# Moving one small sum later in a matmul queue, and taking another from split parts

## The chip, the cores and the metric

The kernel runs on one core of a Trainium2 chip. The metric is device microseconds (us) of one execution. The core's engines work from queues of their own and meet at semaphores: TensorE (PE for the matmuls, PEld for loading their stationary operand), VectorE (DVE), ScalarE (ACT), GpSimd (POOL) and SyncE (SP, which issues the transfers here). "PE waits for a semaphore" means that everything behind that wait in PE's queue stands still too.

## What is computed

Two layers of a decoder trunk over 256 tokens of width 1024, in float32:

```python
for i in range(2):
    x = x + 0.5 * swiglu(rms_norm(x, ffn1_norm[i]), ffn1_w_in[i], ffn1_w_out[i])
    hm = rms_norm(x, mix_norm[i])
    if i == 0: x = x + retention(hm, ret_w_in[0], ret_w_out[0])       # 4 heads, keys 256 wide, values 512
    else:      x = x + window_attention(hm, k_sh, v_sh, ...)          # 16 query heads of 64, window 128
    x = x + 0.5 * swiglu(rms_norm(x, ffn2_norm[i]), ffn2_w_in[i], ffn2_w_out[i])
    if i == 0: k_sh, v_sh = shared_kv(x, kv_norm, kv_w, k_norm)
```

`rms_norm` needs the sum of squares of each token. Inside retention each head's output is normed again by its own sum of squares (over 512 values) and gated before the output projection, which has 16 row blocks of 128: four blocks for each head.

## The kernel before

**Split operands.** Every large product is done as float32r matmuls on two parts. An operand v becomes `hi = v` rounded to float32r and `lo = v - hi`; a product is hi*hi + hi*lo + lo*hi. The activations lie as `[hi | lo]`, 512 columns, so one block of weights costs two matmuls: `w_hi` against 512 columns and `w_lo` against the first 256. The document calls these two a *pair* (`weight_block`, L1213). In *passes* means all the `w_hi` matmuls of a run first and then all of its `w_lo` ones.

**Weights.** They come in units through four slots. SP loads unit u into `stage`, ACT writes `w_hi` (`split`, L337), DVE writes `w_lo` (`split`, L652, 128x2048, one unit). ACT may write a slot only after PE has used the unit four before it (`used`).

**Norm sums.** POOL squares the tiles of x and adds them up (`square_sum`). For the norms in `PARTS` it then writes the sum as `sq_parts = [hi | lo]` (`sum_parts`: a cast, L1179, and a subtraction, L1181), and PE sums over partitions with one float32r matmul against ones. The attention's norm (ATT) isn't in `PARTS`: there PE needs the sum by token as a column, and takes it from the float32 `sq_sum` with two float32 matmuls of two columns each (four records in the trace, because a float32 matmul is two).

**The end of retention.** DVE adds up the last head's squares and writes `sq_parts` (`last_head_sum`, L969 to L974). PE sums them over partitions (`head_sum(4)`), DVE reads that (`norm_y`, L982 on), norms and gates the head, ACT writes the hi part of `y_t`, DVE the lo part (`store_y`, L998, which sets `y_lo`). Meanwhile PE does what doesn't need this head: the first 12 blocks of output tiles 0, 1 and 2 and the first 7 of tile 3 (`early`), with `head_sum(4)` behind the first tile's 12. Then it waits for `y_lo` and finishes tiles 0 to 7 in order. Tiles 0 to 3 use weight units 0 to 3 of this phase; units 4 to 7 follow in the same slots.

**The start of attention.** PE does the keys' transposes, query products, masks, the norm's column sums (`norm_sum(ATT)`) and then transposes, scores and further query products, in an order that is written out by hand in `attention` (PE). DVE, in its own written order, adds the residual tiles, splits a unit (L652), rotates the first half's queries (`q_rope(0, 1)`, L841 to L847), reads the column sums (`token_columns`, L890), computes the head scales and the softmax front (L901 to L1032, twice), splits a unit, rotates the next quarter (`q_rope(0, 0)`) and so on. PE's `q_transposes(c, t)` wait for `roped`, which `q_rope` sets.

Instructions on a matmul helper all have its line, L1211.

Of the kernel before, what the change touches and what calls it, by code (L numbers as in the profile page):

```python
# [21 lines left out]
F32R = mybir.dt.float32r  # L22
# [6 lines left out]
P = 128  # L29
T = 256  # L30
D = 1024
# [9 lines left out]
HEADS_R, DK, DV = 4, 256, 512  # L41
# [45 lines left out]
RET, ATT = 1, 4  # L87
LATE_NORMS = (0, 5)
HEAD_SUMS = HEADS_R
PARTS = {RET: 0, 2: HEADS_R + 1, 3: HEADS_R + 2, 5: HEADS_R + 3}  # L90
CREDIT = 2


def sums_before(m):

    return m + (HEAD_SUMS if m > RET else 0)


def added_for(m):

    return DT * (m + 1) + (HEAD_SUMS if m > RET else 0)
# [22 lines left out]
def trunk(nc, x_t, gains, w_in, w_out, w_ret, w_ret_out, w_kv, w_q, w_o, rot, decay, rope, head_gains,  # L124
          mask_c, sinks_c, ident_c, out):
    def at(name, shape, dtype, offset):
        return nc.alloc_sbuf_tensor_at(name, shape, dtype, offset=offset)
# [54 lines left out]
    ones = at("ones", [P, P], F32, misc + 19968)  # L182
# [3 lines left out]
    sq_sum = at("sq_sum", [P, T], F32, misc + 23552)  # L186
    sq = at("sq", [P, T], F32, misc + 24576)
    sq_parts = at("sq_parts", [P, 2 * T], F32R, misc + 23552)
    sq_all = at("sq_all", [P, T], F32, misc + 27200)
# [8 lines left out]
    ps = nc.alloc_psum_tensor("ps", [P, 8, 512], F32)  # L198
    SUM, FIRST_SUM, COLUMNS = 7, 3, 6
# [45 lines left out]
    def quarter(d):  # L245

        return d // 4, slice(d % 4 * UNIT // 4, (d % 4 + 1) * UNIT // 4)
# [22 lines left out]
    with nc.Block() as block:  # L270
# [371 lines left out]
        def _(dve):  # L642
# [25 lines left out]
            def token_sums(m):  # L668


                dve.wait_ge(sum_done, sums_before(m) + 1)
                bank = FIRST_SUM if m in LATE_NORMS else SUM
                if m == 3:
                    nc.vector.tensor_scalar(col_v[:], ps[:, COLUMNS, 0:4], V_SCALE / D, V_SCALE * EPS, ALU.mult, ALU.add)
                ins = nc.vector.tensor_scalar(n_v[:], ps[:, bank, 0:T], V_SCALE / D, V_SCALE * EPS, ALU.mult, ALU.add)
                if m in PARTS:
                    ins = add_half(ins, PARTS[m], D, bank)
                ins.then_inc(sum_read, 1)

            def token_scale(m):  # L680
# [8 lines left out]
            def add_half(ins, n, width, bank=SUM):  # L689

                ins.then_inc(half_added, 1)
                dve.wait_ge(half_added, n + 1)
                return nc.vector.scalar_tensor_tensor(n_v[:], ps[:, bank, T:2 * T], V_SCALE / width, n_v[:], ALU.mult,
                                                      ALU.add)
# [428 lines left out]
            for d in range(DT):  # L1123
                s, cols = quarter(d)
# [7 lines left out]
            for q in range(2):  # L1132
# [5 lines left out]
                cols = slice(q * UNIT // 2, (q + 1) * UNIT // 2)  # L1138
# [13 lines left out]
        def _(pool):  # L1152
            def square_sum(m):
# [4 lines left out]
                nc.gpsimd.tensor_tensor(sq_sum[:], x[:, 0, :], x[:, 0, :], ALU.mult).then_inc(sum_added, 1)  # L1158
                with pool.Fori(0, DT - 2 if m in PARTS else DT - 1) as i:

# [6 lines left out]
                    nc.gpsimd.tensor_tensor(sq_sum[:], sq_sum[:], sq[:], ALU.add).then_inc(sum_added, 1)  # L1167
                if m in PARTS:
                    pool.wait_ge(sum_added, added_for(m) - 1)
# [3 lines left out]
                    nc.gpsimd.tensor_tensor(sq_all[:], sq_sum[:], sq[:], ALU.add).then_inc(sq_added, 1)  # L1173
                    sum_parts(PARTS[m])

            def sum_parts(n):

                pool.wait_ge(sq_added, n + 1)
                nc.gpsimd.tensor_copy(sq_parts[:, 0:T], sq_all[:]).then_inc(sq_hi, 1)  # L1179
                pool.wait_ge(sq_hi, n + 1)  # L1180
                nc.gpsimd.tensor_tensor(sq_parts[:, T:2 * T], sq_all[:], sq_parts[:, 0:T].bitcast(F32),  # L1181
                                        ALU.subtract).then_inc(sum_added, 1)
# [26 lines left out]
        def _(pe):  # L1209
            def matmul(out_, w, x_, start, stop):  # L1210
                return nc.tensor.matmul(out_, w, x_, start=start, stop=stop)  # L1211
# [7 lines left out]
            def high_product(bank, slot, b, moving, first):  # L1219

                return matmul(ps[:, bank, :], w_hi[:, slot, b * P:(b + 1) * P], moving, first, False)

            def low_product(bank, slot, b, moving, last):

                return matmul(ps[:, bank, 0:T], w_lo[:, slot, b * P:(b + 1) * P], moving[:, 0:T], False, last)
# [15 lines left out]
            def norm_sum(m):  # L1241


                pe.wait_ge(sum_added, added_for(m))
                bank = FIRST_SUM if m in LATE_NORMS else SUM
                if m in PARTS:
                    last = matmul(ps[:, bank, :], ones[:].bitcast(F32R), sq_parts[:], True, True)
                elif m != ATT:
                    last = matmul(ps[:, bank, 0:T], ones[:], sq_sum[:], True, True)
                if m == 3:  # L1250
                    last = column_sums(ps[:, COLUMNS, 0:4], sq_all)
                if m == ATT:
                    last = column_sums(ps[:, SUM, T:T + 4], sq_sum)
                last.then_inc(sum_done, 1)

            def column_sums(out_, sums):

                for t in range(2):
                    last = matmul(out_[:, 2 * t:2 * t + 2], sums[:, t * P:(t + 1) * P], ones[:, 0:2], True, True)
                return last  # L1260

            def first_blocks(kt):

# [208 lines left out]
            def ret_out_in_passes(d, ks):  # L1472

                u = FIRST["ret_out", 0] + d
                pe.wait_ge(hi_ready, u + 1)
                for k in ks:
                    high_product(d, u % SLOTS, k, y_t[:, k, :], k == 0)
                pe.wait_ge(lo_ready, u + 1)
                for k in ks:
                    low_product(d, u % SLOTS, k, y_t[:, k, :], k == YT - 1)  # L1480

            def ret_out(d, ks):

                u = FIRST["ret_out", 0] + d
                pe.wait_ge(lo_ready, u + 1)
                for k in ks:
                    last = weight_block(d, u % SLOTS, k, y_t[:, k, :], k == 0, k == YT - 1)
                return last

            def retention():  # L1490
                with pe.Fori(0, 2) as i:
                    ret_head(0, i)
                    ret_head(1, i)
                three = YT - YT // HEADS_R
                early = (three, three, three, 7, 0, 0, 0, 0)

                pe.wait_ge(pair_free, 4 + 4 * HEADS_R)
                pe.wait_ge(y_lo, HEADS_R - 1)
                ret_out_in_passes(0, range(0, three - 4))
                ret_out(0, range(three - 4, three))  # L1500
                head_sum(HEADS_R)
                for d in range(1, 4):
                    ret_out(d, range(early[d]))

                pe.wait_ge(y_lo, HEADS_R)
                for d in range(DT):
                    ret_out(d, range(early[d], YT)).then_inc(used, 1)
# [272 lines left out]
```

## Time and profile before

| | |
|---|---|
| median of 3 runs | 1016.08 us (1015.81 to 1016.28) |
| the profiled execution | 1016.55 us, of which 1014.8 us from its first to its last instruction |
| PE busy | 1010.3 us |
| PEld busy | 886.1 us |
| DVE busy | 786.3 us |
| ACT busy | 496.7 us |
| POOL busy | 101.1 us |

The page gives each engine's busy time; the chain of work that ended last names, step by step, what the end waited for. A timeline lists instructions by start; neighbours of the same line and operands are merged, with their count as x2, x8. The interval from one matmul's start to the next one's is what a matmul costs PE; the recorded duration is longer, since matmuls are pipelined.

### The profile page before, as it was taken

The numbers are of one execution on the slowest core, as the hardware profiler recorded it, in microseconds if no ns is written. First come the engines' busy times: TensorE is split into PE (matmuls) and PEld (weight loads), VectorE is DVE, ScalarE is ACT, GpSimd is POOL, SyncE is SP. The second block draws the span as 40 slices with busy tenths as digits, with TensorE's granted clock in tenths as the row PEclk, the third lists the DMA queues.
The fourth block names the chain that finished last, engine by engine and source line by source line (L and its number), as shares of the span: only waits on it lengthen the run. The fifth ranks groups of instructions, "written<-read, shape, count | busy, mean of one in ns | idle before, by whom it ended". The sixth has DMA issues, their size and how long they took to land.

```text
span 1014.8 us, 15813 instructions
## 1 busy us (share of the span) xinstructions
PE 1010.3 (100%) x5914; PEld 886.1 (87%) x5914; DVE 786.3 (77%) x886; ACT 496.7 (49%) x536; POOL 101.1 (10%) x103
## 2 busy tenths in 40 slices
PE   9999999999999999999999999999999999999998
PEld 8888888888888888888888888888897898888888
DVE  7988866797797878777767797787778977977743
ACT  7455435544443364454444454465447944554432
POOL 0000013201101052000013100000220041000000
PEclk9999999999999999999999999999999999999999
DMA  9664456652552544554455645535563345544461
GB/s 350 239 233 180 142 174 216 243 202 104 218 193 98 192 175 163 208 200 170 148 189 197 249 165 195 192 140 171 185 239 120 107 160 192 207 170 163 156 191 65
DMA packets 32295, 185.31 MB, mean 183 GB/s; under 512 B 3840, under 2 KB 6400, under 8 KB 16128
## 3 DMA queue, kind: packets, MB, share of 16 engines
q1 hardware_dynamic: 31968, 184.64, 51.0%
q8 instruction: 23, 0.38, 0.2%
q10 hardware_dynamic: 288, 0.16, 0.1%
q14 instruction: 16, 0.13, 0.0%
HBM read 183.73 MB, written 1.05 MB: 182 GB/s over the span
## 4 chain that ended last, share of the span: by engine, by line
PE 100%; issue 0%; DVE 0%; DVEq 0%
PE ps L1211 99%; PE ps L1576 1%; PE ps L1543 0%; PE ps L1535 0%; DVE x L835 0%; DVE ones L1122 0%; DVEq L1121 0%; DVEq L1120 0%; DVEq L1119 0%; DVEq L1118 0%; DVEq L1117 0%
## 5 line engine op out<-in xcount | busy, mean ns | idle before, releaser
L1211 PE MATMUL ps<-h,w_hi 128*128 128x512 f32 x1664 | 556.2, 393 | 0.0
L1211 PE MATMUL ps<-h,w_lo 128*128 128x256 f32 x1664 | 430.6, 279 | 0.0
L652 DVE TENSOR_TENSOR w_lo<-stage,w_hi 128x2048 fp32r<-128x2048 f32 (+1 forms) x190 | 398.4, 2106 | 31.0 <-ACT w_hi L337 30.8
L1211 PEld LDWEIGHTS ps<-h,w_hi 128*128 128x128 f32 x1664 | 310.1, 188 | 67.1 <-issue 0.2
L337 ACT ACTIVATE w_hi<-stage 128x2048 fp32r<-128x2048 f32 (+1 forms) x190 | 326.8, 1727 | 6.0 <-PE ps L1211 5.2
L1211 PEld LDWEIGHTS ps<-h,w_lo 128*128 128x128 f32 x1664 | 301.9, 189 | 3.5
L1211 PE MATMUL ps<-act_t,w_hi 128*128 128x512 f32 (+1 forms) x726 | 240.0, 386 | 0.0
L1211 PE MATMUL ps<-act_t,w_lo 128*128 128x256 f32 x704 | 190.0, 279 | 0.0
L1211 PEld LDWEIGHTS ps<-act_t,w_hi 128*128 128x128 f32 x726 | 134.4, 188 | 28.5
L369 ACT ACTIVATE tmp<-ps 128x1024 f32<-128x1024 f32 x44 | 45.1, 1026 | 190.5 <-PE ps L1211 190.5
L1211 PEld LDWEIGHTS ps<-act_t,w_lo 128*128 128x128 f32 x704 | 130.3, 189 | 0.3
L734 DVE TENSOR_TENSOR tmp<-ps,tmp 128x1024 f32<-128x1024 f32 x44 | 53.8, 1223 | 68.9 <-ACT tmp L369 68.9
L402 ACT ACTIVATE tmp<-ps 128x256 f32<-128x256 f32 x39 | 14.8, 380 | 119.1 <-PE ps L1211 119.1
L1211 PE MATMUL ps<-w_hi,h 128*128 128x512 f32 x192 | 60.4, 396 | 0.0
L780 DVE SCALAR_TENSOR_TENSOR tmp<-ps,tmp 128x256 f32<-128x256 f32 x39 | 16.4, 422 | 54.1 <-ACT tmp L402 54.1
L374 ACT ACTIVATE tmp<-tmp 128x512 f32<-128x512 f32 x44 | 27.9, 633 | 61.1 <-DVE tmp L740 61.1
L740 DVE TENSOR_TENSOR tmp<-tmp,r_row 128x1024 f32<-128x1024 f32 x44 | 53.9, 1225 | 1.5
L1158 POOL TENSOR_TENSOR sq_sum<-x 128x256 f32<-128x256 f32 x5 | 3.1, 614 | 477.4 <-DVE x L782 414.3
L1167 POOL TENSOR_TENSOR sq_sum<-sq_sum,sq 128x256 f32<-128x256 f32 x31 | 45.3, 1460 | 2.4
L1211 PE MATMUL ps<-y_t,w_hi 128*128 128x512 f32 x128 | 44.6, 399 | 0.0
L1211 PEld LDWEIGHTS ps<-w_hi,h 128*128 128x128 f32 x192 | 35.1, 188 | 7.8 <-issue 0.7
L709 DVE SCALAR_TENSOR_TENSOR h<-x,gain,h 128x256 fp32r<-128x256 f32 (+1 forms) x48 | 32.5, 677 | 10.2 <-ACT h L348 10.2
(171 smaller groups left out, 746.8 us busy)
## 6 DMA issues: line engine op xcount, KB each, us to landing
stage<-w_in_dram SPq DMA_DIRECT2D x85, 1024.0 KB, 4.8
stage<-w_out_dram SPq DMA_DIRECT2D x64, 704.0 KB, 4.0
stage<-w_ret_dram SPq DMA_DIRECT2D x24, 1024.0 KB, 4.8
stage<-w_ret_out_dram SPq DMA_DIRECT2D x8, 1024.0 KB, 4.8
stage<-w_q_dram SPq DMA_DIRECT2D x4, 1024.0 KB, 5.5
stage<-w_o_dram SPq DMA_DIRECT2D x4, 1024.0 KB, 4.8
stage<-w_in_dram SPq DMA_DIRECT2D x8, 256.0 KB, 4.1
stage<-w_in_dram SPq DMA_DIRECT2D x2, 512.0 KB, 6.0
```

What stands on the lines that cost most here:

```text
L337: nc.scalar.activation(w_hi[:, s, 0:n], stage[:, s, 0:n], ACT.Copy).then_inc(hi_ready, 1)
L369: nc.scalar.activation(t, ps[:, 4 * (g % 2):4 * (g % 2) + 4, T:2 * T], ACT.Copy).then_inc(in_lo_half, 1)
L374: nc.scalar.activation(tmp[:, g % 2, 0:512], tmp[:, g % 2, 0:512], ACT.Silu).then_inc(in_silu, 1)
L402: nc.scalar.activation(tmp[:, d % 2, 0:T], ps[:, bank, T:2 * T], ACT.Copy, scale=scale).then_inc(out_lo_half, 1)
L652: nc.vector.tensor_tensor(w_lo[:, s, 0:n], stage[:, s, 0:n], w_hi[:, s, 0:n].bitcast(F32), ALU.subtract).then_inc(lo_ready, 1)
L709: nc.vector.scalar_tensor_tensor(h[:, ds(d + per * i, 1), T:2 * T], x[:, ds(d + per * i, 1), :], gain[:, ds(m * DT + d + per * i, 1)], h[: ...
L734: nc.vector.tensor_tensor(t, ps[:, 4 * (g % 2):4 * (g % 2) + 4, 0:T], t, ALU.add).then_inc(in_free, 1)
L740: nc.vector.tensor_tensor(t, t, same(r_row[:], 4), ALU.mult).then_inc(in_scaled, 1)
L780: chain.step(nc.vector.scalar_tensor_tensor(t, ps[:, bank, 0:T], scale, t, ALU.mult, ALU.add))
L1167: nc.gpsimd.tensor_tensor(sq_sum[:], sq_sum[:], sq[:], ALU.add).then_inc(sum_added, 1)
L1211: return nc.tensor.matmul(out_, w, x_, start=start, stop=stop)
L1576: last = nc.tensor.transpose(ps[:, P_T_BANKS[e][r], q * P:(q + 1) * P], s[:, h0 + head, kb * P:(kb + 1) * P], ident[:])
```

## The change

`head_sum(4)` moves from behind tile 0's 12 blocks to behind tile 0's 12 and tile 1's first 4. All of tile 0's 12 blocks are done in passes; before, 8 were in passes and 4 in pairs. Tile 3 has 10 blocks ahead of the wait for `y_lo`, before 7. The attention's norm joins `PARTS`: POOL adds the cast and the subtraction for it, and PE's column sums are four float32r matmuls of two columns on `sq_parts` (two token halves, hi and lo part each), accumulated by token half. The other norms' column sums (norm 3) stand as they were, written in place.

```diff
-PARTS = {RET: 0, 2: HEADS_R + 1, 3: HEADS_R + 2, 5: HEADS_R + 3}
+PARTS = {RET: 0, 2: HEADS_R + 1, 3: HEADS_R + 2, ATT: HEADS_R + 3, 5: HEADS_R + 4}
...
                 if m in PARTS:
-                    ins = add_half(ins, PARTS[m], D, bank)
+                    ins = add_half(ins, PARTS[m] - (m > ATT), D, bank)
...
-                if m in PARTS:
+                if m == ATT:
+                    for t in range(2):
+                        for part in range(2):
+                            cols = slice(T * part + P * t, T * part + P * (t + 1))
+                            last = matmul(ps[:, SUM, T + 2 * t:T + 2 * t + 2], sq_parts[:, cols],
+                                          ones[:, 0:2].bitcast(F32R), part == 0, part == 1)
+                elif m in PARTS:
                     last = matmul(ps[:, bank, :], ones[:].bitcast(F32R), sq_parts[:], True, True)
-                elif m != ATT:
+                else:
                     last = matmul(ps[:, bank, 0:T], ones[:], sq_sum[:], True, True)
...
-                if m == ATT:
-                    last = column_sums(ps[:, SUM, T:T + 4], sq_sum)
...
                 three = YT - YT // HEADS_R
-                early = (three, three, three, 7, 0, 0, 0, 0)
+                early = (three, three, three, 10, 0, 0, 0, 0)
...
-                ret_out_in_passes(0, range(0, three - 4))
-                ret_out(0, range(three - 4, three))
+                ret_out_in_passes(0, range(early[0]))
+                ret_out(1, range(4))
                 head_sum(HEADS_R)
-                for d in range(1, 4):
+                ret_out(1, range(4, early[1]))
+                for d in range(2, 4):
                     ret_out(d, range(early[d]))
```

## Rows read from the trace of the kernel before

**Rows 1.** The page, parts 1 and 4: busy time; the chain's shares.

```profile
PE 1010.3 (100%) x5914; PEld 886.1 (87%) x5914; DVE 786.3 (77%) x886; ACT 496.7 (49%) x536; POOL 101.1 (10%) x103
...
PE 100%; issue 0%; DVE 0%; DVEq 0%
```

**Rows 2.** Timeline, end of retention (start, duration, engine, line, operation, count, idle before).

```profile
339.54 2.09 PE L1211 MATMUL ps<-y_t,w_hi 128*128 128x512 f32 x8
...
343.83 0.50 PE L1211 MATMUL ps<-sq_parts,ones 128*128 128x512 f32 x1
...
344.17 0.39 PE L1211 MATMUL ps<-y_t,w_hi 128*128 128x512 f32 x1
```

**Rows 3.** Timeline, a sum from parts for which PE doesn't wait.

```profile
393.57 0.40 PE L1211 MATMUL ps<-sq_parts,ones 128*128 128x512 f32 x1
...
393.81 0.40 PE L1211 MATMUL ps<-h,w_hi 128*128 128x512 f32 x1
```

**Rows 4.** Timeline, PE, passes of eleven blocks in the second FFN's output.

```profile
746.59 2.68 PE L1211 MATMUL ps<-act_t,w_hi 128*128 128x512 f32 x11
...
749.11 1.48 PE L1211 MATMUL ps<-act_t,w_lo 128*128 128x256 f32 x11
...
750.42 2.68 PE L1211 MATMUL ps<-act_t,w_hi 128*128 128x512 f32 x11
```

**Rows 5.** Timeline, the last head's lo part, and PE's first pair behind the wait.

```profile
352.97 1.23 DVE L998 TENSOR_TENSOR y_t<-y_f,y_t 128x1024 fp32r<-128x1024 f32 x1 [1.20 <-ACT y_t L503]
...
355.12 0.40 PE L1211 MATMUL ps<-y_t,w_hi 128*128 128x512 f32 x1
```

**Rows 6.** Timeline, weight units 4 and 5 of the projection, and PE's first pair of tile 4.

```profile
356.74 1.92 ACT L337 ACTIVATE w_hi<-stage 128x2048 fp32r<-128x2048 f32 x1 [3.87 <-PE ps L1211]
358.69 2.29 DVE L652 TENSOR_TENSOR w_lo<-stage,w_hi 128x2048 fp32r<-128x2048 f32 x1 [4.49 <-ACT w_hi L337]
...
362.54 0.40 PE L1211 MATMUL ps<-y_t,w_hi 128*128 128x512 f32 x1
...
364.42 2.29 DVE L652 TENSOR_TENSOR w_lo<-stage,w_hi 128x2048 fp32r<-128x2048 f32 x1 [0.79 <-ACT w_hi L337]
```

**Rows 7.** Timeline, POOL's last steps of a norm that is in PARTS, and DVE beside them.

```profile
389.34 0.61 POOL L1171 TENSOR_TENSOR sq<-x 128x256 f32<-128x256 f32 x1 [3.92 <-DVE x L782]
...
391.40 0.74 POOL L1181 TENSOR_TENSOR sq_parts<-sq_all,sq_parts 128x256 fp32r<-128x256 f32 x1
391.58 2.71 DVE L652 TENSOR_TENSOR w_lo<-stage,w_hi 128x2048 fp32r<-128x2048 f32 x1 [1.32 <-ACT w_hi L337]
```

**Rows 8.** Timeline, start of attention: the last square, DVE's split and rotation, the column sums.

```profile
759.78 0.61 POOL L1164 TENSOR_TENSOR sq<-x 128x256 f32 x1 [6.18 <-DVE x L782]
...
761.98 2.29 DVE L652 TENSOR_TENSOR w_lo<-stage,w_hi 128x2048 fp32r<-128x2048 f32 x1 [1.30 <-ACT w_hi L337]
...
764.27 0.69 DVE L841 TENSOR_TENSOR q_a<-ps,tables 128x512 f32<-128x512 f32 x1
...
765.81 0.50 PE L1211 MATMUL ps<-ones,sq_sum 128*128 128x2 f32 x4
...
766.17 0.72 PE L1211 MATMUL ps<-w_hi,h 128*128 128x512 f32 x2
```

**Rows 9.** Timeline, attention further on: the next split and rotation, and the transposes behind them.

```profile
773.53 2.28 DVE L652 TENSOR_TENSOR w_lo<-stage,w_hi 128x2048 fp32r<-128x2048 f32 x1
...
775.73 0.68 DVE L841 TENSOR_TENSOR q_a<-ps,tables 128x512 f32<-128x512 f32 x1
...
777.11 0.69 DVE L847 TENSOR_TENSOR q_a<-q_a,q_b 128x512 f32<-128x512 f32 x1
...
777.75 0.39 PE L1211 MATMUL ps<-w_lo,h 128*128 128x512 f32 x1
...
777.91 0.42 PEld L1543 LDWEIGHTS ps<-ident,q_a 128*128 128x128 f32 x4 [0.20 <-issue]
777.97 0.60 PE L1543 MATMUL ps<-ident,q_a 128*128 128x128 f32 x4
```

More of the change, by code:

```diff
@@ L1245, in norm_sum @@
                 bank = FIRST_SUM if m in LATE_NORMS else SUM
-                if m in PARTS:
+                if m == ATT:
[5 more added lines that the diff above has]
+                elif m in PARTS:
                     last = matmul(ps[:, bank, :], ones[:].bitcast(F32R), sq_parts[:], True, True)
-                elif m != ATT:
+                else:
                     last = matmul(ps[:, bank, 0:T], ones[:], sq_sum[:], True, True)
                 if m == 3:
-                    last = column_sums(ps[:, COLUMNS, 0:4], sq_all)
-                if m == ATT:
-                    last = column_sums(ps[:, SUM, T:T + 4], sq_sum)
+                    for t in range(2):
+                        last = matmul(ps[:, COLUMNS, 2 * t:2 * t + 2], sq_all[:, t * P:(t + 1) * P], ones[:, 0:2],
+                                      True, True)
                 last.then_inc(sum_done, 1)
[L1256 to L1260, printed above, removed]
             def first_blocks(kt):
```

## The prediction

> **What bounds the kernel now.** Read the page first [rows 1]: PE is busy for 1010.3 of 1014.8 us, and the chain of work that ended last is PE for 100% of the span. No transfer and no other engine sets the end. So a change is worth what it takes from PE's queue: matmuls that cost less from start to start, and gaps in which PE stands before a wait. An edit on DVE, ACT or POOL is worth nothing unless PE waits for it, and then it costs just what PE waits. I therefore read two stretches of the timeline, the end of retention [rows 2 to 6] and the start of attention [rows 7 to 9], each for the same thing: when does a value get ready, and when does PE ask for it.
>
> A unit for what follows. From the pair behind the head's sum, 344.17, to the first pair of tile 4, 362.54 [rows 2, 6], PE does 31 + 21 = 52 pairs: 18.37 / 52 = 0.353 us a pair.
>
> **Part 1, the last head's sum moved back.** Now the sum starts at 343.83 and the next matmul at 344.17, 0.34 later [rows 2]. Where PE needn't wait, the same matmul costs 0.24 [rows 3]. So the wait costs 0.10. In the new order the sum stands 4 blocks later: the four blocks in passes cost what rows 4 show for eleven, (750.42 - 746.59) / 11 = 0.348 each, so it starts at 343.83 + 4 x 0.348 = 345.22. Its data were what PE waited for just before 343.83, 1.4 us earlier: the wait is gone for certain. Four blocks that go from pairs to passes give 4 x (0.353 - 0.348) = 0.02. Sum of the part: -0.12 us.
>
> What is late next. The sum comes 1.39 later, so the last head's lo part does too. It is done now at 352.97 + 1.23 = 354.20 [rows 5], 10.37 after the sum's start; then at 345.22 + 10.37 = 355.59. PE reaches its wait for it now at 344.17 + 31 x 0.353 = 355.12, the row in the group: 0.92 to spare. In the new order 8 + 12 + 10 = 30 pairs lie behind the sum: 345.22 + 0.24 + 30 x 0.353 = 356.06. To spare: 0.47. No wait, so the three more pairs of tile 3 do cover it; without them PE would stand 0.6 us.
>
> Behind that wait, tile 0 is finished 0.94 later than now (356.06 against 355.12), and with it unit 0's slot comes free, for which ACT waits to write unit 4 [rows 6]. The pairs that moved ahead lie in front of this release. Unit 4 is whole now at 358.69 + 2.29 = 360.98 and asked for at 362.54; then at 361.92, asked for at 356.06 + 18 x 0.353 = 362.42. Spare 1.56 becomes 0.50. Unit 5 behind it: now at 364.42 + 2.29 = 366.71; then 367.65, asked for 16 pairs later, at 368.07: 0.42. From unit 6 on DVE's pace is under PE's for a tile of 16 pairs (5.65 us), so spares grow. The same 0.94 shifts the next norm's sum: its parts are done at 391.40 + 0.74 = 392.14 [rows 7], then 393.08, while PE asks at 393.57 - 0.12 = 393.45 [rows 3]: 0.37 left. Each of these edits costs nothing as long as its spare holds; all four spares (0.37 to 0.50) are positive, yet none is large. The move passes no transfer on any queue.
>
> **Part 2, column sums from split parts, on PE.** Now four records: first at 765.81, the next product's first matmul at 766.17, which with its neighbour takes 0.72 [rows 8], where two of 0.39 at a step of 0.22 to 0.23 [rows 9] make 0.62: 0.36 + 0.10 = 0.46, or 0.115 each. Afterwards again four weight loads and four matmuls of two columns. A float32r load in front of two columns isn't in the trace. The nearest rows: passes of `w_lo`, one load and 256 columns, (750.42 - 749.11) / 11 = 0.119 each, 4 x 0.119 = 0.48 [rows 4]; the transposes, four loads in a row, whose three steps take (0.42 - 0.14) / 3 = 0.09, 4 x 0.09 = 0.37 [rows 9]. So between -0.09 and +0.02; I take 0, since count and size of the loads stay and loads, not columns, fill this stretch.
>
> **Part 2, on POOL and DVE.** Here lies the cost. POOL now ends the norm with its addition. The cast and the subtraction come behind it. In a norm that is in PARTS the subtraction starts 391.40 - 389.34 = 2.06 after the last square [rows 7]; for attention that is 759.78 + 2.06 = 761.84, until 762.58 [rows 8]. PE asks for the sum at 765.81: three us to spare, so PE doesn't wait for POOL. But DVE starts a split at 761.98, inside the subtraction. In rows 7 the same two stand the same way: subtraction 391.40 to 392.14, split from 391.58, 0.56 of overlap, and the split takes 2.71 where it takes 2.28 elsewhere [rows 9]: +0.43. (Two other norms show the same pair, at 193.81 and 572.28.) Here the overlap is 762.58 - 761.98 = 0.60, so +0.47.
>
> The Trainium skill (SBUF — State Buffer, Who interferes with whom) says that a DVE instruction with two SBUF inputs and a GpSimd one that reads SBUF share a port pair as an exclusive lock: who starts first holds it, the other is fully blocked. The rows agree that the later one pays, with 0.43 of 0.56, so not all of the overlap. By the rule in full the split would lose 0.60.
>
> Who is queued behind the split on DVE: the first rotation, at 764.27 [rows 8]. A following instruction can start 0.08 before the split's recorded end (773.53 + 2.28 = 775.81 against 775.73 [rows 9]); here it started at the end itself, so 0.08 was slack. The delay is 0.47 - 0.08 = 0.39. From there DVE's chain to the second rotation is one instruction behind the other (the head scales, two softmax fronts, the split of 773.53), so the 0.39 arrives at 777.11, where the rotation ends at 777.80. PE's transposes wait for just this. Their load starts at 777.91, behind an idle 0.20 of PEld, and the first matmul at 777.97, which is 0.22 after the last one, 777.75, its usual step [rows 9]. So PE loses nothing there now, and has next to nothing to spare: at most 0.06, from load to matmul. A delay of 0.39 costs PE 0.33 to 0.39; I take 0.37. The transposes before (at 767) wait for the first rotation too; their load is some 0.1 us late then, under the matmul in front of it, so I put them at 0. Further on DVE, ACT and PE are all late by the same amount, so their waits for each other neither grow nor pay it back, and the end of the kernel is PE's.
>
> **Sum.** -0.12 + 0 + 0.37 = +0.25 us. The profiled execution took 1016.55 us, 1014.8 of it the span; that run would be 1016.80. It lies 0.47 above the median of the three runs, 1016.08, from which I count: 1016.08 + 0.25 = 1016.33, given as 1016.3. A measurement of this kernel can tell about 0.2%, 2 us, from no change; the forecast is no change that can be told, by eight times.
>
> **Rivals.** *DVE's delay doesn't reach PE.* The overlap may miss (the two begin 0.14 apart), or there is slack in the chain up to 777 that I don't see. Then part 1 is left: 1016.08 - 0.12 = 1015.96. For it: PE's queue shows only 0.20 of idle loading there. Against it: three norms show the overlap without exception. Chance 0.20.
>
> *DVE is held for the whole overlap.* A split held until the subtraction ends loses 0.60; the delay is 0.60 - 0.08 = 0.52, PE loses 0.50, the time is 1016.08 - 0.12 + 0.50 = 1016.46. Against it: 0.43 of 0.56 in rows 7. Chance 0.08. This is what the rule of the Trainium skill (SBUF — State Buffer, Who interferes with whom) gives in full.
>
> *Slower: weight units 4 and 5 come late at the end of retention.* The release of unit 0's slot moves back by 0.94 and eats the spare of both units down to 0.50 and 0.42 [rows 6]. From half a microsecond on every further one is PE's, one for one. If DVE takes unit 4 one split's length (2.29) later, behind the head's last steps, PE stands 2.29 - 0.50 = 1.79 and the time is 1016.33 + 1.79 = 1018.1, over 0.2% slower. Against it: DVE has been idle for 4.49 when unit 4's split starts [rows 6], so nothing of that length stands before it. Chance 0.04.
>
> That the change doesn't do what it says (the sum still waits) is excluded by 1.4 us.
>
> **How the numbers follow.** Forecast 0.66, the three rivals 0.20, 0.08 and 0.04; 0.02 is left for what I don't see, half of it a gain. All but the third rival and that rest lie within 0.2%: same 0.94, slower 0.05, faster 0.01. The range: the first rival less half of the runs' spread (0.25), 1015.7, up to the second rival with the same spread and the open cost of a spare that fails by a few tenths, 1017.0. The column sums' bounds (-0.09, +0.02) lie inside.
>
> **What would show it.** Part 1: the sum from parts at 345.2 with 0.24 to the next matmul, no idle PEld before it; no PE gap at 356.1, 362.4 or before the next norm's sum. Part 2: a subtraction of POOL at 761.7 (all of it 0.12 earlier), a split beside it of 2.75 instead of 2.29, the rotation 0.39 later against the square, and at 778 an idle PEld of 0.55 to 0.6 with a step of 0.6 instead of 0.22 from the last product to the transposes. What would make it wrong: a split of 2.29 there, or the step at 778 unchanged (then the first rival), or idle PEld at the first pair of tile 4 or 5 (then the third).

## The result, and the profile after

| | before | after |
|---|---|---|
| median | 1015.92 us of 22 | 1022.72 us of 22 |
| range | 1015.29 to 1017.06 | 1016.04 to 1023.23 |
| profiled execution | 1016.55 us | 1016.77 us |

The changed kernel is slower: the ratio is 1.0051, 95% interval 1.0039 to 1.0062. Its times do not scatter around one value, they fall into three groups: 6 lie at 1016.0 to 1016.8, one at 1019.84, 15 at 1022.5 to 1023.2. The kernel before has one group only. The granted clock of TensorE is 1.0 (its 2.4 GHz level) in every execution of either, so the groups are not a matter of the clock.

The profiled execution is one of the short group. It is read first, because it holds the whole of what the prediction worked on; a long one follows with the experiments. Page of after, parts 1 and 4:

```profile
PE 1010.1 (100%) x5914; PEld 885.9 (87%) x5914; DVE 786.7 (78%) x886; ACT 496.7 (49%) x536; POOL 102.6 (10%) x105
...
PE 91%; DVE 6%; ACT 2%; issue 1%; POOL 0%; ACTq 0%; DVEq 0%; POOLq 0%
```

Against [rows 1] the busy times hardly move, but the chain that ended last is no longer PE's alone: 6% of it is DVE and 2% ACT. So somewhere PE now stood behind them. Timeline of after at the end of retention, with the lines that answer to [rows 2, 5, 6]:

```profile
345.44 0.40 PE L1211 MATMUL ps<-sq_parts,ones 128*128 128x512 f32 x1
345.68 0.40 PE L1211 MATMUL ps<-y_t,w_hi 128*128 128x512 f32 x1
...
354.49 1.22 DVE L998 TENSOR_TENSOR y_t<-y_f,y_t 128x1024 fp32r<-128x1024 f32 x1 [1.20 <-ACT y_t L503]
356.09 0.39 PE L1211 MATMUL ps<-y_t,w_hi 128*128 128x512 f32 x1
...
359.62 2.29 DVE L652 TENSOR_TENSOR w_lo<-stage,w_hi 128x2048 fp32r<-128x2048 f32 x1 [3.92 <-ACT w_hi L337]
362.33 0.39 PE L1211 MATMUL ps<-y_t,w_hi 128*128 128x512 f32 x1
```

The sum starts without an idle load, 0.24 ahead of the next matmul. From 356.09 to 362.33 PE does 18 pairs: 6.24 / 18 = 0.347 us a pair. The prediction had 0.353 for them, from [rows 2, 6]. PE asks for no value here before it is ready: the last head's lo part ends at 355.71 against 356.09, unit 4 at 361.91 against 362.33.

At the next norm's sum it does. Timeline of after there, with the lines that answer to [rows 3, 7]:

```profile
392.37 0.75 POOL L1181 TENSOR_TENSOR sq_parts<-sq_all,sq_parts 128x256 fp32r<-128x256 f32 x1
392.54 2.72 DVE L652 TENSOR_TENSOR w_lo<-stage,w_hi 128x2048 fp32r<-128x2048 f32 x1 [1.32 <-ACT w_hi L337]
392.82 0.28 PE L1211 MATMUL ps<-h,w_lo 128*128 128x256 f32 x1
393.17 0.19 PEld L1211 LDWEIGHTS ps<-sq_parts,ones 128*128 128x128 f32 x1 [0.39 <-POOL sq_parts L1181]
393.17 0.50 PE L1211 MATMUL ps<-sq_parts,ones 128*128 128x512 f32 x1
393.51 0.39 PE L1211 MATMUL ps<-h,w_hi 128*128 128x512 f32 x1
...
395.19 0.41 DVE L675 TENSOR_SCALAR n_v<-ps 128x256 f32<-128x256 f32 x1
395.63 0.42 DVE L693 SCALAR_TENSOR_TENSOR n_v<-ps,n_v 128x256 f32<-128x256 f32 x1
...
396.29 0.19 PEld L1211 LDWEIGHTS ps<-h,w_hi 128*128 128x128 f32 x1 [0.16 <-issue]
396.29 0.49 PE L1211 MATMUL ps<-h,w_hi 128*128 128x512 f32 x1
396.63 0.28 PE L1211 MATMUL ps<-h,w_lo 128*128 128x256 f32 x1
```

POOL's parts are done at 393.12, 0.04 from the predicted 393.08. But PE, whose last product before the sum starts at 392.82, would have begun the sum at 392.94, not at the predicted 393.45. So PEld is idle for 0.39, and PE loses 393.17 - 392.94 = 0.23 in front of the sum and 0.34 - 0.24 = 0.10 behind it. A second, shorter wait follows at the start of the next group of products, 396.29: PE's queue waits there until DVE has read the sum (L675 and L693, done at 396.05), and that reading stands on DVE behind a split that began at 392.54. The profile names no releaser for this wait; the order of the kernel does, and an experiment below removes it. PE's step there is 0.34, where it is 0.23 beside it: 0.11 more.

Timeline of after, start of attention and further on, with the lines that answer to [rows 8, 9]:

```profile
761.61 0.75 POOL L1181 TENSOR_TENSOR sq_parts<-sq_all,sq_parts 128x256 fp32r<-128x256 f32 x1
761.78 2.72 DVE L652 TENSOR_TENSOR w_lo<-stage,w_hi 128x2048 fp32r<-128x2048 f32 x1 [1.32 <-ACT w_hi L337]
764.43 0.68 DVE L841 TENSOR_TENSOR q_a<-ps,tables 128x512 f32<-128x512 f32 x1
...
765.62 0.50 PE L1211 MATMUL ps<-ones,sq_parts 128*128 128x2 f32 x4
765.99 0.72 PE L1211 MATMUL ps<-w_hi,h 128*128 128x512 f32 x2
...
771.75 0.16 DVE L1032 TENSOR_TENSOR sm<-sinks,sm 128x4 f32<-128x4 f32 x1
771.83 1.22 DVE L1028 TENSOR_REDUCE sm<-ps 128x4 f32<-128x1024 f32 x1
...
777.15 0.69 DVE L847 TENSOR_TENSOR q_a<-q_a,q_b 128x512 f32<-128x512 f32 x1
777.56 0.39 PE L1211 MATMUL ps<-w_lo,h 128*128 128x512 f32 x1
777.95 0.42 PEld L1544 LDWEIGHTS ps<-ident,q_a 128*128 128x128 f32 x4 [0.43 <-issue]
777.98 0.63 PE L1544 MATMUL ps<-ident,q_a 128*128 128x128 f32 x4
```

The four float32r column sums cost what the four float32 records cost (0.37 to the next product, before 0.36). The split takes 2.72 instead of 2.29, and PE's step to the transposes at 777.98 is 0.42 instead of 0.22.

None of this is 6 us. In this short execution the losses (0.23 + 0.10 + 0.11 + 0.20) stand against a PE that came to the next norm's sum early, and the time is near the old one. The question is what the 16 longer ones do.

### The profile page after: what moved, and what is told of

It is laid out like the page before. It is cut to its first block, busy times and chain, and to the rows that moved or that the text cites. A ratio compares the mean times of both kernels' runs of the same rounds, so it can differ in the third digit from the quotient of the medians.

```text
span 1014.9 us, 15810 instructions
## 1 busy us (share of the span) xinstructions
PE 1010.1 (100%) x5914; PEld 885.9 (87%) x5914; DVE 786.7 (78%) x886; ACT 496.7 (49%) x536; POOL 102.6 (10%) x105
## 3 DMA queue, kind: packets, MB, share of 16 engines
HBM read 183.73 MB, written 1.05 MB: 182 GB/s over the span
## 4 chain that ended last, share of the span: by engine, by line
PE 91%; DVE 6%; ACT 2%; issue 1%; POOL 0%; ACTq 0%; DVEq 0%; POOLq 0%
PE ps L1211 90%; DVE w_lo L652 3%; ACT w_hi L337 1%; DVE x L782 0%; ACT s_two L530 0%; DVE h L709 0%; DVE sm L1028 0%; DVE tmp L780 0%; PE ps L1577 0%; DVE hs L901 0%; DVE q_a L847 0%; DVE q_a L841 0%; DVE q_b L844 0%; DVE hs L666 0%; DVE hs L664 0%
```

## Experiments

**The same kernel again.** No edit; twelve executions in one run, and one profiled execution in another.

> The changed kernel once more, for a profile of one of its long executions. Its times fall into two groups, near 1016.3 and near 1022.9 us, with one at 1019.8. Theory P (pace): in the long ones PE does a pair of matmuls in 0.3534 us instead of 0.3467 for some 1000 pairs, from the norm sum at 393 us up to the shared keys and values at 740: 1000 x 0.0067 = 6.7 us, with no wait that explains it. Theory W (a wait): PE stands at one or a few places for 6.7 us in all, at a weight unit that lands or is split late. Theory A (attention): the 6.7 us lie between 757 and 825 us, where part 2 works.

> The changed kernel a third time, for the profile of a long execution. P and Q: at 1019.5 or 1022.9 us the pairs take 0.3534 us from 580 to 740 us or from 393 to 740 us, and nothing else differs by more than 0.2 us. At 1016.2 us: 0.3467 throughout.

Measured: 4 executions at 1016.1 to 1016.5, 3 at 1019.4 to 1020.3, 5 at 1022.5 to 1023.3 (ratio 1.0042, 1.0026 to 1.0058), so the groups belong to the program and not to one session. The single execution of the second run took 1022.79 and is a long one. Busy time by stretch (columns: stretch, its length, busy time and count of PE, PEld, DVE, ACT, POOL, granted clock, DMA share, GB/s), first the short execution of after, then the long one:

```profile
345.00:385.00 40.00, 40.00 (x232) 35.22 (x231) 31.66 (x40) 17.13 (x21) 17.30 (x12) 1.00 0.41 150
400.00:570.00 170.00, 170.00 (x983) 149.87 (x982) 129.63 (x115) 78.72 (x72) 15.10 (x13) 1.00 0.52 182
590.00:730.00 140.00, 140.00 (x809) 122.44 (x809) 109.72 (x102) 68.64 (x68) 8.46 (x7) 1.00 0.54 186
```

```profile
400.00:570.00 170.00, 170.00 (x964) 147.49 (x963) 126.65 (x112) 78.29 (x70) 15.09 (x13) 1.00 0.52 179
590.00:730.00 140.00, 140.00 (x794) 121.35 (x793) 108.75 (x101) 69.19 (x68) 6.50 (x7) 1.00 0.52 179
```

PE is busy for all of both stretches, at clock 1.00, but in the long execution it gets 964 matmuls through where the short one gets 983, and 794 instead of 809. The start times say how: a pair of `w_hi` (512 columns) and `w_lo` (256) takes 0.3467 us in the one and 0.3534 us in the other, pair after pair. From 393 to norm 3's sum at 577 the 1.9% are 184 x 19 / 983 = 3.6 us; from there to 740, 163 x 15 / 809 = 3.0 us. Together 6.6, the distance of the outer groups, and each half is the distance of the middle one.

The idle loads of the two executions are nearly the same: POOL's parts with 0.4 us once in either, and 0.2 us more in the long one, at 9 us. Where the paces part is seen in the long one's timeline, PE at the start of the group behind norm 2's sum:

```profile
395.51 0.39 PE L1211 MATMUL ps<-h,w_hi 128*128 128x512 f32 x1
395.74 0.28 PE L1211 MATMUL ps<-h,w_lo 128*128 128x256 f32 x1
395.86 0.49 PE L1211 MATMUL ps<-h,w_hi 128*128 128x512 f32 x1
396.19 0.28 PE L1211 MATMUL ps<-h,w_lo 128*128 128x256 f32 x1
396.31 0.39 PE L1211 MATMUL ps<-h,w_hi 128*128 128x512 f32 x1
...
396.66 0.40 PE L1211 MATMUL ps<-h,w_hi 128*128 128x512 f32 x1
396.90 0.28 PE L1211 MATMUL ps<-h,w_lo 128*128 128x256 f32 x1
397.02 0.40 PE L1211 MATMUL ps<-h,w_hi 128*128 128x512 f32 x1
```

The sum was late in both, and up to 395.86 both go at 0.347. Then comes the second wait (step 0.33), and behind it three pairs take 0.35, 0.36 and 0.35, 1.06 together, and stay so. Nothing waits any more; the slow pace simply goes on for hundreds of pairs.

**The two parts apart.** Each alone on the kernel before: the new order in retention with its `early` counts, and the PARTS edit with its column sums.

> Part 1 alone (the retention's order new, the attention's column sums as before). P: the sum of norm 2 still comes out of a wait for POOL near 393 us, so both groups of times stay, each about 0.3 us lower than with both parts (1016.0 and 1022.6). A: one group, at 1015.9. W: one or both groups, and the wait is where the order was changed.

> Part 2 alone (the retention's order as before). P: PE finds norm 2's sum ready at 393 us, as in the kernel before, so there is one group of times, at 1016.0 + 0.3 = 1016.3 us, the 0.3 being PE's longer idle time ahead of the transposes at 778 us. A: two groups, 1016.3 and 1022.9. W: one group.

Part 1 alone: 1018.96 to 1019.50 four times and 1022.33, ratio 1.0039 (1.0026 to 1.0052). Part 2 alone: 11 executions in one group, 1015.53 to 1016.62, median 1016.24 against 1016.01, ratio 1.0002 (0.9993 to 1.0010), as was expected. So the groups, and the loss, come from part 1; the rival by which they come from attention falls. Part 1's profiled execution, 1018.96, is of the middle group: fast to 577, slow from there (same view and columns as above):

```profile
400.00:570.00 170.00, 170.00 (x983) 148.69 (x982) 129.20 (x115) 79.29 (x73) 15.62 (x14) 1.00 0.53 184
590.00:730.00 140.00, 140.00 (x794) 121.43 (x793) 108.81 (x100) 68.02 (x66) 8.44 (x7) 1.00 0.53 181
```

**A wait, put into the kernel before.** Norm 2's sum one row block earlier, where POOL isn't done.

```diff
-                        if g == 0 and kt == 5 and m not in LATE_NORMS:
+                        if g == 0 and kt == (4 if m == 2 else 5) and m not in LATE_NORMS:
```

> The kernel before with norm 2's sum behind the fifth row block of the second FFN's first group instead of the sixth: PE asks for POOL's parts at about 392.0 us, 0.2 before they are there, so it waits, and nothing else of the change is in. P: this wait alone lets the high group appear (1022.7 in some executions, 1016.0 to 1016.2 in the others); if the length of the wait decides, one group at one of these. A and W: one group at 1016.1 (the wait's 0.2 us more than before).

Measured: 4 at 1016.3 to 1016.8, 6 at 1019.8 to 1020.4, 2 at 1022.8 and 1023.5; ratio 1.0029 (1.0017 to 1.0042). Its profiled execution (1022.83) shows the wait and the slow pace from it on; a list of PEld's and PE's records:

```profile
391.66 0.19 PEld L1211 LDWEIGHTS ps<-sq_parts,ones 128*128 128x128 f32 x1 [0.63 <-POOL sq_parts L1181]
391.99 0.39 PE L1211 MATMUL ps<-h,w_hi 128*128 128x512 f32 x1
...
393.05 0.40 PE L1211 MATMUL ps<-h,w_hi 128*128 128x512 f32 x1
```

Three pairs in 1.06: 0.353. So the groups, some 3 and 6 us apart, appear without either part of the change. That the wait alone makes them isn't shown: the edit also puts the sum right behind the row blocks in passes, where it stood four pairs later, and no run parts the two.

**The waits taken out of the changed kernel.** Norm 2's sum is moved behind row block 6, and the reading of it (`token_sums(2)`) stands on DVE ahead of the split that had delayed it.

```diff
-                        if g == 0 and kt == 5 and m not in LATE_NORMS:
+                        if g == 0 and kt == (6 if m == 2 else 5) and m not in LATE_NORMS:
...
+                if n == RET and d == DT - 1:
+                    token_sums(2)
...
                 if f in (1, 2):
-                    token_sums(m)
+                    if f == 2:
+                        token_sums(m)
```

> The changed kernel with the wait at norm 2 taken out: its sum stands one row block later (kt 6), 1.39 us, where POOL's parts are ready, and DVE reads it before it splits the last unit, so that the next group needn't wait either. P: out of a sum for which PE doesn't wait the pairs always go on at 0.3467 us; one group of times, at 1016.3 - 0.7 = 1015.6 us (the waits of 0.39 and 0.16 and what they add to the matmuls around them go). A rival, that a pace of 0.3534 comes by chance wherever the order of retention is new: two or three groups up to 1022.9.

> The kernel with norm 2's sum one row block later again, for the profile of one of its short executions (7 of 11 lay at 1015.6 to 1016.5 us, 4 above 1019). Q: the sum stands behind 8 pairs there, so the slow cycle goes on behind it in every execution; in the short ones something behind the sum, ahead of 400 us, must break the cycle. If the sum itself is followed by 0.3467 in the short ones, its position isn't what decides.

One group near 1015.6 was expected, and it didn't come. Of 11 executions 7 lie at 1015.6 to 1016.5, but 2 at 1019 and 2 at 1022. The single one was meant to show a short execution and took 1019.15, so what a short one does here isn't known. Ratio 1.0017 (1.0004 to 1.0030). That is better than the changed kernel, and neither profiled execution has an idle load at the sum, yet both go slowly from the sum on. So waits are not the whole of it. What else the edit changed is the sum's place: 8 pairs behind the row blocks in passes, before 4.

**An attempt to restore the pace.** The changed kernel with its first wait, with row block 6 in passes and one more matmul of 512 columns behind the sum (its product is overwritten by the real one; it only takes time).

> The changed kernel with its wait at norm 2 left in, but behind it the next row block (kt 6) is done in passes and then comes one more matmul of 512 columns, for which PE doesn't wait; its product goes to a bank that the next group overwrites. P: whatever pace the wait left, a matmul that stands alone without a wait sets 0.3467 again, as the sum does at 345 us; one group, at 1016.3 + 0.25 = 1016.5 us. If a wait itself costs the 6.7 us, or the pace is a property of the execution: the groups stay at 1016.5, 1019.8 and 1023.1.

It missed: 1022.64 to 1023.54 in all five, ratio 1.0074 (1.0060 to 1.0088). In its profile the pairs behind the added matmul go at 0.353. The second wait is gone here, so the slow pace doesn't need it. But this doesn't show that no such matmul can restore the pace: the edit also puts a run in passes behind the sum, and the added matmul stands right behind that run. What a run in passes leaves is seen further on.

**Norm 3's columns ahead of its sum,** in the changed kernel: the four float32 records at 577 swap places with the float32r sum.

> The changed kernel with norm 3's two column sums ahead of its sum over partitions instead of behind it (577 us). P: the sum then stands alone right in front of the pairs and sets the pace of 0.3467 there, so what lies behind 577 us no longer keeps the slow pace: the highest group falls from 1022.9 by some 480 pairs x 0.0067 = 3.2 to 1019.7, the middle one joins the lowest at 1016.3. If norm 3 has no part in it: groups at 1016.3, 1019.6 and 1022.9 as before.

Measured: two at 1015.95 and 1015.98, five at 1019.2 to 1020.0, none near 1023, which it was meant to remove; ratio 1.0026 (1.0013 to 1.0039). The middle group stayed, though, and its profiled execution, 1019.34, has x983 and x795 in the two stretches above: it is slow just behind 577, which the edit was to make fast. So the highest group went, but not for the reason given, and why it went is open. A different order at this one place doesn't keep the pace up.

**The place of a sum for which PE doesn't wait.** Two edits of the kernel before. One has the last head's sum one pair later (5 pairs behind the passes instead of 4), the other norm 2's sum one pair later (also 5 instead of 4). Neither meets a wait.

```diff
                 ret_out(0, range(three - 4, three))
+                ret_out(1, range(1))
                 head_sum(HEADS_R)
-                for d in range(1, 4):
+                ret_out(1, range(1, early[1]))
+                for d in range(2, 4):
```

> The kernel before with the last head's sum only one pair later and nothing else of the change: tile 3 keeps its 7 blocks, the column sums stay as they were. P: PE doesn't wait for this sum (its data come 0.35 us before it is asked for), so the pairs behind it run at 0.3467 instead of 0.3534 us, 116 x 0.0067 = 0.78, and 0.1 of waiting goes; weight units and norm 2's parts come 0.3 us earlier than before, so norm 2's sum finds them ready. One group, at 1016.0 - 0.9 = 1015.1 us. If the pace behind the sum isn't set there: 1015.9.

```diff
+                                if g == 0 and m == 2 and kt == 6 and o == 0:
+                                    norm_sum(m)
-                        if g == 0 and kt == 5 and m not in LATE_NORMS:
+                        if g == 0 and kt == 5 and m != 2 and m not in LATE_NORMS:
```

> The kernel before with norm 2's sum one pair later, behind 5 pairs instead of 4; nothing waits more than before, nothing else is changed. Q: the sum takes the place of the 0.236 step of the cycle, the slow cycle goes on from 393 to at least 577 us (530 pairs x 0.0067 = 3.5), and to 740 us if norm 3's sums leave it so (6.7): one or two groups, at 1019.4 and 1022.6 us, with no wait at all. If only waits lead to the slow pace: one group at 1015.9.

The first was expected to gain (1015.1) and missed: 1016.02 to 1016.77, ratio 1.0006 (0.9997 to 1.0015). Its profiled execution has the sum without a wait at 343.86 and the slow pace behind it, in 345 to 385 at least, where the fast one was expected. By medians it is 0.50 longer than the kernel before, though the 0.1 of waiting is gone. From this came the thought that the place itself matters, and the second edit was made to try it. It came out as expected: 10 of 12 executions at 1018.8 to 1019.8, two at 1016.0 and 1016.5, ratio 1.0028 (1.0019 to 1.0036). A shift of one matmul by one pair costs 3.5 us (median 1019.28 against 1015.75). Its PE around the sum, and the two stretches:

```profile
393.35 0.28 PE L1211 MATMUL ps<-h,w_lo 128*128 128x256 f32 x1
393.47 0.40 PE L1211 MATMUL ps<-sq_parts,ones 128*128 128x512 f32 x1
393.71 0.39 PE L1211 MATMUL ps<-h,w_hi 128*128 128x512 f32 x1
...
394.76 0.40 PE L1211 MATMUL ps<-h,w_hi 128*128 128x512 f32 x1
```

```profile
400.00:570.00 170.00, 170.00 (x964) 147.36 (x963) 126.01 (x112) 78.30 (x70) 15.09 (x13) 1.00 0.51 179
590.00:730.00 140.00, 140.00 (x810) 122.41 (x810) 111.56 (x103) 70.51 (x68) 8.47 (x7) 1.00 0.52 180
```

The sum follows its predecessor by 0.12 and is followed after 0.24: no stall at all. Yet the three pairs behind it take 1.05, and PE is slow until norm 3's sum, which here happens to bring the fast pace back. In [rows 3] the same matmul, one pair earlier, leaves the fast pace.

The step from such a sum to the next matmul, in thousandths from the records' start times, sorts the places. Over the profiled executions a sum met without a wait at the head or at norm 2 has a step of 0.240 or 0.241 in 16 places, all behind 1 or 4 pairs, and the fast pace follows in all 16. It has 0.236 in 4 places, all behind 5 or 8 pairs, and the slow pace follows in all 4. In two more places it has 0.230, behind 4 pairs that are at the fast pace already; that pace goes on there, in one of them (the next kernel) only for four pairs. Pairs behind a run in passes mostly go in a cycle of three (`w_hi` steps of 0.233, 0.241 and 0.236, with their `w_lo` steps 1.06 together, which is the slow pace), so 1 and 4 pairs are the same phase of it, and so are 5 and 8. In these places, then, the slow pace is what a run in passes leaves, and a sum at the first of the two phases turns it into the fast one.

**Four pairs again between the passes and the sum, and no wait.** The kernel without waits from above, with row block 5 in passes too, so that only block 6's four pairs lie ahead of norm 2's sum.

```diff
-                                        else m == 2 and kt <= 4)
+                                        else m == 2 and kt <= (5 if g == 0 else 4))
```

> The changed kernel without the waits at norm 2, as e5, and with the sixth row block in passes too, so that norm 2's sum stands behind 4 pairs instead of 8. Q: a sum behind 4 pairs is followed by 0.3467, and no wait disturbs it: one group of times, near 1015.8 us. If long executions come from something else than the sum's position and the waits there: groups at 1016, 1019 and 1022 as in e5.

It missed as well: 1019.16 to 1019.46 three times, 1022.12 and 1022.41, ratio 1.0049 (1.0036 to 1.0062). In its profile the pairs ahead of the sum and behind it are fast at first; at 395.42, the next group's start, one `w_hi` step is 0.25 instead of 0.23, with no idle load shown, and the slow cycle begins there. So the phase at the sum doesn't settle what comes later. That this hesitation of 0.02 us brought the slow pace is likely, but it is one execution and isn't shown.

**The second wait alone taken out.** The changed kernel, with its late sum, but with `token_sums(2)` ahead of the split, so that the next group's banks are free in time.

```diff
+                if n == RET and d == DT - 1:
+                    token_sums(2)
...
                 if f in (1, 2):
-                    token_sums(m)
+                    if f == 2:
+                        token_sums(m)
```

> The changed kernel with norm 2's sum where it was (PE waits 0.39 us for POOL's parts) but DVE reading it before it splits the last unit, so that the second wait, at the next group's start 3 us later, goes. Q: the first wait leaves one of three cycles; groups at 1015.9, 1019.2 and 1022.5 remain in other shares. If the second wait alone decides: one group at 1015.9.

Measured: 10 of 12 at 1015.8 to 1016.7, one each at 1019.10 and 1023.04, ratio 1.0014 (1.0002 to 1.0026). The first wait is still there (0.37 at 393.25), the second is gone, and the short group is 10 of 12 where the changed kernel, over its three runs, has 10 of 35. The traces agree: the six profiled executions that have this first wait with pairs right behind it all go on at 0.347 up to the next group, whatever their time. So in the changed kernel it is mostly the second, smaller wait that leaves the slow pace up to 577; two long executions show that it isn't the only way.

**The change's gain without its waits.** The kernel before with tile 0's 12 blocks in passes and the head's sum behind only one pair of tile 1; tile 3 keeps 7 blocks. Once without, once with part 2.

```diff
-                ret_out_in_passes(0, range(0, three - 4))
-                ret_out(0, range(three - 4, three))
+                ret_out_in_passes(0, range(early[0]))
+                ret_out(1, range(1))
                 head_sum(HEADS_R)
-                for d in range(1, 4):
+                ret_out(1, range(1, early[1]))
+                for d in range(2, 4):
```

> The kernel before with all twelve blocks of tile 0 in passes, one pair of tile 1 and then the last head's sum; tile 3 keeps 7 blocks and the column sums stay as they were. Theory Q (position, the successor of P): behind passes the pairs run in a cycle of three (steps of 0.241 + 0.120, 0.236 + 0.113, 0.233 + 0.117); a sum that takes the place of the 0.241 step, that is one behind 1, 4 or 7 pairs, is followed by pairs of 0.3467, one behind 2, 5 or 8 pairs by the cycle of 0.3534; a wait in front of it leaves either. Here one pair lies between: 0.3467 from 344 to 385 us, 0.8 less than with the slow cycle, 0.1 of waiting gone, unit 4 and norm 2's parts 0.3 earlier, no wait there. One group, at 1015.1 us. If the position has no part: 0.3534 as in the kernel with 8 + 4 + 1 pairs, one group at 1016.0.

> The same order with part 2 of the change (attention's column sums from split parts). Q: one group, the order's time plus part 2's 0.2 to 0.3 us, 1015.1 + 0.3 = 1015.4. If part 2 takes part in the groups: 1016 and above 1019.

Without part 2: 11 executions in one group, median 1015.55 against 1015.85, ratio 0.9994 (0.9985 to 1.0003). The sum waits no more, PE keeps 0.347 from it on, and there is no wait at norm 2. It is the fastest version here, though the interval doesn't part it from the kernel before. With part 2: one group, median 1015.87, ratio 1.0000 (0.9991 to 1.0009). So part 2 costs 0.32 by medians, which is within the noise of either. The traces of the two agree: PE's step to the transposes is 0.23 without it and 0.44 with it, 0.21 more.

## Why the prediction was wrong

**The step that failed** is the unit at its start: "18.37 / 52 = 0.353 us a pair". It took one pace, that of a stretch that went slowly behind a wait [rows 2, 6], as what a pair costs. The trace of before held the other one too, behind the sum for which PE didn't wait: ten pairs from 393.81 [rows 3] take 3.47. Timeline of before:

```profile
397.28 0.39 PE L1211 MATMUL ps<-h,w_hi 128*128 128x512 f32 x1
```

The slow stretch was also chance. Three other profiled executions have the old order of retention and a wait at the head's sum (step 0.327), and all three go on at 0.347 behind it. Busy time by stretch, before and part 2 alone:

```profile
345.00:385.00 40.00, 40.00 (x228) 34.74 (x227) 31.56 (x40) 18.08 (x22) 18.15 (x13) 1.00 0.43 155
345.00:385.00 40.00, 40.00 (x232) 34.97 (x231) 31.75 (x40) 18.12 (x22) 18.22 (x13) 1.00 0.45 159
```

This fits the two experiments that move the head's sum. The slow pace from the head's sum to norm 2's costs 0.78 us (worked out below the table). If one execution in four of the kernel before pays that, as in these four, always going slowly but without the wait costs 0.75 x 0.78 - 0.10 = 0.48 us, and never going slowly gains 0.25 x 0.78 + 0.10 + 0.02 = 0.31. The medians gave 0.50 (the sum one pair later) and 0.30 (behind twelve blocks in passes and one pair), the means 0.54 and 0.47. The share is an estimate from four executions.

In the new order the head's sum isn't stalled, and the pairs behind it go at 0.347. So PE comes to each value earlier than was worked out, and the spares shrink:

| value | spare predicted | spare in after |
|---|---|---|
| last head's lo part | 0.47 | 356.09 - 355.71 = 0.38 |
| unit 4 | 0.50 | 362.33 - 361.91 = 0.42 |
| unit 5 | 0.42 | 362.33 + 16 x 0.3467 - 367.66 = 0.22 |
| norm 2's sum | 0.37 | 392.94 - 393.12 = -0.18 |

When the values were ready was forecast to 0.1 us (parts at 393.12 for 393.08, unit 4 at 361.91 for 361.92); only when PE came for them was not. "Each of these edits costs nothing as long as its spare holds" is true, and the fourth didn't hold. The prediction called the spares small, and its range had room for one that fails by a few tenths, but in the sum their error stood at nothing: between the head's sum and norm 2's PE needs 392.94 - 345.68 = 47.26, some 7 of it for 20 blocks in passes, the rest 40.3 / 0.3467 = 116 pairs, and 0.0067 on each is 0.78 us, twice the smallest spare. Seen from its own start PE is indeed 0.22 + 0.51 = 0.73 early: the head's sum starts 0.22 after the predicted time, and PE reaches norm 2's 0.51 ahead of it.

**The second failure** is that no rival had a matmul pace in it. Even with the wait of norm 2 foreseen, the working would have added some 0.4 us; a pace that a wait leaves behind for 350 us wasn't in the sum or the range. That it is the pace is shown by the counts: of the 17 profiled executions of all these kernels, the 8 below 1017 us go at 0.347 in both long stretches (400 to 570 and 590 to 730), the 5 between 1018.9 and 1019.7 at 0.353 in one of them, and the 4 between 1022.0 and 1022.9 in both. What sets the pace is known less well: a shift without a wait costs 3.5 us, and the removal of the second wait turns most executions short.

**Part 1's own gain** was right in mechanism: no wait at the head's sum, 0.24 to the next matmul. The sum starts at 345.44 here, at 344.91 and 345.02 in the other two profiled executions of the kernel; predicted was 345.22.

**Part 2 on PE** was put at 0 and is 0.01.

**Part 2 on POOL and DVE** had its mechanism right and its size somewhat high: 0.37 predicted, 0.32 by medians (0.23 for the part alone), 0.20 to 0.21 at PE's step in the traces. The split beside the subtraction takes 2.72 for a predicted 2.75, and the rotation behind it starts 2.65 after the split's start where it was 2.29, so 0.36 late for 0.39. But from the start of this rotation to the start of the next one's last instruction (L847), DVE needs 12.72 instead of 12.84. The 0.12 are the "slack in the chain up to 777" of the first rival, partly: the second softmax front started 0.19 behind its predecessor before and starts 0.08 behind it now (771.75 and 771.83 above), probably because its data had been a little late. The rival was thus partly right.

The Trainium skill (SBUF — State Buffer, Who interferes with whom) calls the shared port pair "an exclusive lock"; by that the later of two such instructions would wait for the whole overlap. Subtraction and split overlap by 762.36 - 761.78 = 0.58 here, and the split is 0.43 longer, as in [rows 7]; the second rival, which rested on the whole overlap, is not borne out.

**Units 4 and 5** were not late, in any profiled execution of the changed kernel.

The short executions are therefore near what was forecast (10 of the 35, 1016.0 to 1016.8), with a loss at norm 2 and a gain of pace that happen to cancel. The forecast described one of three outcomes, and not the commonest.

What stays open: why pairs of one program have two paces at one clock, and which offset at a wait leaves which. Second waits of the changed kernel with the same step (0.332) left the fast pace in one profiled execution and the slow one in another. At norm 3's sum, 577, the pace changes in some executions. There too a step goes with it: from the last record of its column sums to the next product it is 0.314 or 0.315 in the 11 profiled executions that go on fast, and 0.324 or 0.325 in the 5 that go on slowly (the kernel with the columns first left out). What sets that step wasn't found. That 5 or 8 pairs go with the slow pace is seen in 4 places only. Of the two kernels that have them at norm 2, 7 of 11 and 2 of 12 executions were short all the same, and of these none was profiled.

## What to carry to other kernels

Before a spare is worked out over a hundred instructions, take the pace from more than one stretch, and ask which of them the change will leave behind it; the spare has to exceed the count times the difference. Where executions of one program fall into groups, count matmuls in equal stretches of a short and a long one before looking for a wait: equal waits with unequal counts mean a pace. A matmul that is moved or briefly held in a PE-bound queue can cost more than ten times its own length behind it, so a small edit there needs many executions, not one profile.

## What the runs showed of the hardware

Alternating float32r matmuls of 512 and 256 columns, each with its own load, run in these traces at 0.3467 or at 0.3534 us a pair, 2% apart, at granted clock 1.00 and with no idle load between. Either pace held for some 490 pairs (400 to 570 us). The places where it changed were a single matmul of 512 columns between the pairs, a wait of 0.2 us and, in one execution, a hesitation of 0.02 us. The DMA share (0.51 to 0.54 in the two long stretches) doesn't tell the two apart, and the short and the long execution of the changed kernel are one program, so the other engines have the same work. The cause was not found.
